# A two-layer decoder trunk in fp32: the split weights' rows and the low part of x at other offsets in memory

## Chip, cores and metric

One core of a Trainium2 chip (trn2) runs the whole program. The metric is the device time of one execution in microseconds (us), as a median of the runs shown. Engines: PE is TensorE (PEld its weight loads), DVE is VectorE, ACT is ScalarE, POOL is GpSimd, SP is the engine that issues most DMAs.

## What is computed

`x` is 512 tokens by 1024 features, fp32. Two layers, each: RMSNorm, one input projection, two mixers whose outputs are joined, an output projection, residual, RMSNorm, a squared-ReLU MLP of width 4096, residual. Layer 0 mixes with RWKV-7 and gated DeltaNet heads, layer 1 with top-k sparse and block-sparse attention.

```python
h = rms_norm(x, norm1_g[l])
x = x + mixer_l(h @ w_in) @ w_out          # w_in: 1024 x 3856 and 1024 x 2888; w_out: 1024 x 1024
h = rms_norm(x, norm2_g[l])
x = x + square(relu(h @ mlp_w1[l])) @ mlp_w2[l]   # 1024 x 4096, 4096 x 1024
```

## The kernel before

**A product in three passes.** A matmul in float32r keeps fewer bits than fp32, so both operands are split: `hi` is the value rounded to float32r, `lo` the rest. A weight tile times an activation is `w_hi*x_hi + w_lo*x_hi + w_hi*x_lo`. `products` (L535) issues it for the KT = 8 tiles of the contraction: first 8 pairs on the high activation (L542 with `w_hi`, L543 with `w_lo`), then 8 matmuls on the low activation (L547). The weight tile of 128 x 128 is the stationary operand, the 512 tokens are the moving one, and all 24 matmuls of such a group go to one PSUM bank.

**The input projection of layer 0** has weight tiles of 128 columns of its own (31 tiles, `tile` at L556, and `first_tiles` at L563 for two of them, with the same passes at L569, L570 and L574). Operands are `x_hi`, `x_lo`, `pw_hi`, `pw_lo`: PH, PL, PWH and PWL in the code. They are tensors laid over the arena by hand, at word offsets X_HI = 6696, PW_HI = 12968 and X_LO = 46704. An assert in the allocation ties these numbers to the carved regions.

**All later projections** take their weights in units of 256 columns (8 x 256 words in each of 128 partitions; there are 84). SP loads a unit into one of two raw slots (RAW), with rows of USLOT = 264 words. ACT rounds it into `w_hi` (`weight_hi`, L1163), POOL subtracts to get `w_lo` (`weight_lo`, L2313), each in two slots that take turns by `u % 2`, and PE runs one group of 24 matmuls for each half of 128 columns (`split_unit`, L895). ACT may fill a slot of `w_hi` when PE has finished the unit before last, and POOL follows ACT. 264 is there for one unit alone, `u_ikv`, which has 8 columns more. The activations are `a_hi`, `a_lo` (input of the MLP), `h_hi`, `h_lo` (input of the other projections and the hidden layer). In `token_major` (L991) of the value projections the sides are exchanged: the activation is stationary, and the weight rows of 256 or 136 columns move.

**Where the operands lie.** The slots and activations are allocated one behind the other:

```python
AH, AL, HL, HH = (parts(n_, 1, KT, W)[:, 0] for n_ in ("a_hi", "a_lo", "h_lo", "h_hi"))
WH, WL = parts("w_hi", 2, KT, USLOT), parts("w_lo", 2, KT, USLOT)
```

A word is 4 bytes, `lower` has 28224 words ahead of them, and W = 512. Counted from the start of `lower`, in bytes within 512:

| operand | start | step from one k to the next |
|---|---|---|
| a_hi, a_lo, h_lo, h_hi | 256 | 2048 (none within 512) |
| w_hi, w_lo, slot 0 | 256 | 1056 (32 within 512) |
| w_hi, w_lo, slot 1 | 0 | 1056 (32 within 512) |
| x_hi | 160 | 2048 (none) |
| pw_hi, pw_lo | 160 | 512 (none) |
| x_lo | 448 | 2048 (none) |

So the weight tile of step k stands 32*k bytes (plus 256 in slot 1) past the activation's place within 512 bytes, from 0 at k = 0 to 224 at k = 7. For layer 0's input projection that distance is 0 in the high passes, and 288 bytes in the low pass. The second half of a unit, 128 columns on, is 512 bytes further and so at the same place.

**Order of the work.** It is fixed by the program: each engine has its own list, and semaphores join them. PE waits for `lo_ready` before a unit and for `bank_read` before it writes a PSUM bank again; DVE empties the banks.

Of the kernel before, what the change touches and what calls it, by code (L numbers as in the profile page):

```python
# [25 lines left out]
ALU = mybir.AluOpType  # L26
# [71 lines left out]
def trunk_kernel(nc, a, out):  # L98
    ctx = ExitStack()
    with ctx:  # L100
# [1 line left out]
            return ctx.enter_context(nc.semaphore(name))  # L102

        ARENA, PARTS = 53000, 28224
        X_HI, PW_HI, X_LO = 6696, 12968, 46704
        with nc.sbuf_tensor("below_x_hi", [P, X_HI], F32), nc.sbuf_tensor("x_hi", [P, KT, W], F32R) as PH, \
                nc.sbuf_tensor("below_pw", [P, PW_HI - X_HI - KT * W], F32), \
                nc.sbuf_tensor("pw_hi", [P, 3, KT, P], F32R) as PWH, nc.sbuf_tensor("pw_lo", [P, 3, KT, P], F32R) as PWL:
# [9 lines left out]
        def parts(name, a_, n, w):  # L118
            return ctx.enter_context(nc.sbuf_tensor(name, [P, a_, n, w], F32R))

        AH, AL, HL, HH = (parts(n_, 1, KT, W)[:, 0] for n_ in ("a_hi", "a_lo", "h_lo", "h_hi"))
        WH, WL = parts("w_hi", 2, KT, USLOT), parts("w_lo", 2, KT, USLOT)
        ps = ctx.enter_context(nc.psum_tensor("ps", [P, 8, 512], F32))
        bank = [ps[:, i, :] for i in range(8)]

# [3 lines left out]
        def carve(n):  # L129
            off = top[0]  # L130
            top[0] += n
            assert top[0] <= ARENA, top[0]
            return off

        def flat(off, n):

            if off >= PARTS:
                return upper[:, off - PARTS:off - PARTS + n]
            assert off + n <= PARTS, (off, n)
            return lower[:, off:off + n]  # L140
# [66 lines left out]


        SQ_KKS = flat(carve(4 * PW), 4 * W)
        o_pl = carve(KT * W)  # L210
        PRAW = flat(o_ring, 2 * KT * P).rearrange("p (s k n) -> p s k n", s=2, k=KT)
        assert (X_HI, PW_HI, X_LO) == (o_ht, o_ring + 2 * KT * P, o_pl)
# [188 lines left out]
        def unit_cols(u):  # L401
            return USLOT if u == u_ikv else UW

        def as_f32(x):
            return x.bitcast(F32)

        x_rows = a["x"][0].rearrange("(t p) d -> p t d", p=P)

# [103 lines left out]
        def _(pe):  # L512
            def take(q, dyn=0):

                if q >= 8:
                    pe.wait_ge(bank_read, dyn + (q - 7))
                return bank[q % 8]
# [377 lines left out]
            def split_unit(u, q, xh, xl, dyn_u=0, dyn_q=0, waits=None, ks=tuple(range(KT))):  # L895

                pe.wait_ge(lo_ready, dyn_u + (u + 1))
                for b in range(2):
                    cols = slice(b * P, (b + 1) * P)
                    products(take(q + b, dyn_q)[:, :],  # L900
                             [(k, WH[:, u % 2, k, cols], WL[:, u % 2, k, cols], xh[:, k, :], xl[:, k, :])
                              for k in ks], waits if b == 0 else None).then_inc(bank_filled, 1)

            def normed_split(n):
# [17 lines left out]
            def mlp(l):  # L922
                def quarter(i, first):
                    for v in range(first, 4):
                        split_unit(u_mlp[l] + v, q_m1[l] + 2 * v, AH, AL, i * 8, i * 16)

                    hidden = (lambda k: pe.wait_ge(h1_hi, i * 8 + (32 * l + k + 1)),
                              lambda k: pe.wait_ge(h1_ready, i * 8 + (32 * l + 4 + k + 1)))
                    for v in range(4):
                        split_unit(u_mlp[l] + 4 + v, q_m2[l] + 2 * v, HH, HL, i * 8, i * 16,  # L930
                                   hidden if v == 0 else None)

                n, u = 2 * l + 1, u_mlp[l]
                pe.wait_ge(lo_ready, u + 1)
                sums, tile0, tile1 = take(q_norm[n]), take(q_m1[l]), take(q_m1[l] + 1)
                for k in range(KT):
                    pe.wait_ge(h_hi, KT * (n - 1) + k + 1)
                    for b, o in enumerate((tile0, tile1)):
                        cols = slice(b * P, (b + 1) * P)
                        pe.matmul(o[:, :], WH[:, u % 2, k, cols], AH[:, k, :], start=(k == 0), stop=False)  # L940
                        pe.matmul(o[:, :], WL[:, u % 2, k, cols], AH[:, k, :], start=False, stop=False)
                pe.wait_ge(sq_sum, sums_to(n + 1))
                pe.matmul(sums[:, :], ONES, SQ[n][:, 0, :], start=True, stop=True).then_inc(bank_filled, 1)
                for b, o in enumerate((tile0, tile1)):
                    cols = slice(b * P, (b + 1) * P)
                    for k in range(KT):
                        pe.wait_ge(h_lo, KT * (n - 1) + k + 1)
                        mm = pe.matmul(o[:, :], WH[:, u % 2, k, cols], AL[:, k, :], start=False,  # L948
                                       stop=(k == KT - 1))
                    mm.then_inc(bank_filled, 1)  # L950
                quarter(0, 1)
                if l == 0:
                    with pe.Fori(1, 4) as i:
                        quarter(i, 0)
                    return
                with pe.Fori(1, 3) as i:
                    quarter(i, 0)
                for v in range(4):
                    split_unit(u_mlp[l] + v, q_m1[l] + 2 * v, AH, AL, 24, 48)
                hidden = (lambda k: pe.wait_ge(h1_hi, 24 + (32 * l + k + 1)),  # L960
                          lambda k: pe.wait_ge(h1_ready, 24 + (32 * l + 4 + k + 1)))
                for v in range(3):
                    split_unit(u_mlp[l] + 4 + v, q_m2[l] + 2 * v, HH, HL, 24, 48, hidden if v == 0 else None)
                turned_tiles(0, range(4))
                u = u_mlp[l] + 7
                pe.wait_ge(lo_ready, 24 + (u + 1))
                for b in range(2):
                    cols = slice(b * P, (b + 1) * P)
                    products(take(q_m2[l] + 6 + b, 48)[:, :],
                             [(k, WH[:, u % 2, k, cols], WL[:, u % 2, k, cols], HH[:, k, :], HL[:, k, :])  # L970
                              for k in range(KT)]).then_inc(bank_filled, 1)
                    turned_tiles(1, range(2) if b == 0 else range(2, 4))

            def projected(l, xh, xl, waits, ks):
                for v in range(4):
# [9 lines left out]
            keep_busy(take(q_norm[2] + 1)[:, :], 5)  # L985
            u = u_ikv
            pe.wait_ge(lo_ready, u + 1)
            products(take(q_ik)[:, :], [(k, WH[:, u % 2, k, 0:P], WL[:, u % 2, k, 0:P], HH[:, k, :],
                                         HL[:, k, :]) for k in range(KT)], normed_split(2)).then_inc(bank_filled, 1)

            def token_major(o, i, wh, wl):  # L991

                rows = slice(i * P, (i + 1) * P)
                return products(o, [(k, HH[:, k, rows], HL[:, k, rows], wh[:, k, :], wl[:, k, :])
                                    for k in range(KT)])

            for v in range(2):
                o = take(q_v + v)
                for i in range(2):
                    mm = token_major(o[:, i * VIW:(i + 1) * VIW], 2 * v + i, WH[:, u % 2, :, P:USLOT],  # L1000
                                     WL[:, u % 2, :, P:USLOT])
                mm.then_inc(bank_filled, 1)

            def unit_tile(u, b, q):
                cols = slice(b * P, (b + 1) * P)
                pe.wait_ge(lo_ready, u + 1)
                products(take(q)[:, :], [(k, WH[:, u % 2, k, cols], WL[:, u % 2, k, cols], HH[:, k, :], HL[:, k, :])
                                         for k in range(KT)]).then_inc(bank_filled, 1)

            def mv(v):  # L1010
                u = u_mv[v]
                pe.wait_ge(lo_ready, u + 1)
                for i in range(TT):
                    token_major(take(q_mv[v * TT + i])[:, 0:UW], i, WH[:, u % 2, :, 0:UW],
                                WL[:, u % 2, :, 0:UW])\
                        .then_inc(bank_filled, 1)

            def index_products(i):
# [107 lines left out]
        def _(act):  # L1126
# [29 lines left out]
            def weight_hi(u, dyn=0, q_done=None, dyn_q=0):  # L1156


                act.wait_ge(raw_full[u % 2], dyn + raw_count(u))
                if q_done is not None:  # L1160
                    filled(q_done, dyn_q)
                w = unit_cols(u)
                act.activation(WH[:, u % 2, :, 0:w], RAW[:, u % 2, :, 0:w], ACT.Copy).then_inc(hi_ready, 1)  # L1163

            def h_split(n):
                for k in range(KT):
# [1035 lines left out]
        def _(pool):  # L2202
# [106 lines left out]
            def weight_lo(u, dyn=0):  # L2309

                pool.wait_ge(hi_ready, dyn + (u + 1))
                w = unit_cols(u)
                pool.tensor_tensor(WL[:, u % 2, :, 0:w], RAW[:, u % 2, :, 0:w],  # L2313
                                   as_f32(WH[:, u % 2, :, 0:w]), ALU.subtract)\
                    .then_inc(lo_ready, 1)

            def weights(first, last):
# [70 lines left out]
```

## Time and profile before

| | |
|---|---|
| median of 3 runs | 1460.98 us (1460.77 to 1461.29) |
| span of the profiled execution | 1458.6 us |
| what lies around the span, median less span | 2.4 us |
| PE busy | 1426.5 us, 98% of the span |
| PEld busy | 1140.5 us, 78% |
| DVE, ACT, POOL busy | 657.9, 595.2, 524.1 us |
| DMA | 110.06 MB, mean 75 GB/s |

The profile gives no time of its own for the profiled execution beside its span. A row of the page's list of groups names line, engine, operation, output and inputs, shape and count, then busy time, mean ns of one, and idle time before it with what ended it. Matmuls overlap: one is listed with some 390 ns from its start to its modelled end, while the next starts after some 230 ns. What a matmul costs in a full stream is therefore the spacing of the starts, to be read from the timeline, or from the chain of waits, where each matmul stands with the time until the next one took over.

### The profile page before, as it was taken

Reading aid. Unit: us, or ns where it says so; the run is one execution under the profiler, and the core shown is the slowest. Engines: PE = TensorE matmul, PEld = TensorE weight load, DVE = VectorE, ACT = ScalarE, POOL = GpSimd, SP = SyncE. Lnnn points to the kernel's source line nnn. Section 1 sums busy time; section 2 is a strip of 40 time slices with the busy share of each in tenths; the row PEclk is TensorE's granted clock in tenths of the full one; section 3 lists DMA queues with packets and bytes.
Section 4 is the critical chain, followed back from the end, with each engine's and each line's share of the span. In section 5 each row is a group of like instructions: output and inputs, shape, how many; then the busy total and the mean of one; then the engine's idle time right before and its main releaser. Section 6 shows DMA issues by size and latency. Waiting matters only on the chain.

```text
span 1458.6 us, 24642 instructions
## 1 busy us (share of the span) xinstructions
PE 1426.5 (98%) x10331; PEld 1140.5 (78%) x10331; DVE 657.9 (45%) x1090; ACT 595.2 (41%) x849; POOL 524.1 (36%) x239
## 2 busy tenths in 40 slices
PE   7999999999999999999999999999999999999998
PEld 5787778889787888888887767775687888888886
DVE  4665767788743214132133258836443223131231
ACT  5524663444634223133233465568635223131331
POOL 3543322011144334434444224332333533443341
PEclk9999999999999999999999999999999999999999
DMA  5333200000222322233223222210032223223221
GB/s 148 87 101 84 75 15 4 4 4 3 89 87 87 113 90 87 93 97 99 86 87 99 70 63 87 87 58 2 9 106 89 87 87 114 88 86 112 90 87 58
DMA packets 128972, 110.06 MB, mean 75 GB/s; under 512 B 10742, under 2 KB 126576, under 8 KB 128880
## 3 DMA queue, kind: packets, MB, share of 16 engines
q1 hardware_dynamic: 128000, 107.12, 23.7%
q8 instruction: 73, 1.20, 0.4%
q10 hardware_dynamic: 880, 1.59, 0.3%
q14 instruction: 19, 0.16, 0.0%
HBM read 106.60 MB, written 2.10 MB: 75 GB/s over the span
## 4 chain that ended last, share of the span: by engine, by line
PE 91%; DVE 4%; ACT 2%; POOL 1%; issue 1%; DMA 1%; SPq 0%; ACTq 0%; DVEq 0%; POOLq 0%
PE ps L547 24%; PE ps L542 24%; PE ps L543 24%; PE ps L679 5%; PE ps L1070 2%; PE ps L1080 1%; PE ps L1091 1%; PE ps L687 1%; PE ps L579 1%; PE ps L1045 1%; POOL pw_lo L2226 1%; PE ps L694 1%; PE ps L1021 1%; PE ps L656 1%; PE ps L948 1%
## 5 line engine op out<-in xcount | busy, mean ns | idle before, releaser
L2313 POOL TENSOR_TENSOR w_lo<-lower,w_hi 128x2048 fp32r<-128x2048 f32 (+1 forms) x84 | 388.8, 4629 | 551.0 <-ACT w_hi L1163 534.4
L542 PE MATMUL ps<-h_hi,w_hi 128*128 128x512 f32 x792 | 315.2, 398 | 0.9 <-ACT h_hi L1446 0.8
L543 PE MATMUL ps<-h_hi,w_lo 128*128 128x512 f32 x792 | 312.0, 394 | 0.0
L1163 ACT ACTIVATE w_hi<-lower 128x2048 fp32r<-128x2048 f32 (+1 forms) x84 | 160.2, 1907 | 242.8 <-PE ps L547 242.8
L547 PE MATMUL ps<-h_lo,w_hi 128*128 128x512 f32 x792 | 202.2, 396 | 0.5
L542 PE MATMUL ps<-a_hi,w_hi 128*128 128x512 f32 x480 | 189.1, 394 | 0.0
L543 PE MATMUL ps<-a_hi,w_lo 128*128 128x512 f32 x480 | 189.1, 394 | 0.0
L542 PEld LDWEIGHTS ps<-h_hi,w_hi 128*128 128x128 f32 x792 | 148.6, 188 | 41.7 <-issue 5.4
L547 PEld LDWEIGHTS ps<-h_lo,w_hi 128*128 128x128 f32 x792 | 148.7, 188 | 38.0 <-DVE h_lo L1770 2.5
L543 PEld LDWEIGHTS ps<-h_hi,w_lo 128*128 128x128 f32 x792 | 148.7, 188 | 35.6 <-issue 1.2
L2054 DVE TENSOR_TENSOR lower<-lower,ps 128x512 f32<-128x512 f32 x64 | 44.0, 687 | 275.4 <-PE ps L547 275.4
L2038 DVE SCALAR_TENSOR_TENSOR lower<-ps,lower 128x512 f32<-128x512 f32 x64 | 44.3, 692 | 226.0 <-PE ps L547 209.9
L1433 ACT ACTIVATE lower<-lower 128x512 f32<-128x512 f32 x64 | 40.5, 633 | 215.9 <-DVE lower L2038 215.9
L547 PE MATMUL ps<-a_lo,w_hi 128*128 128x512 f32 x480 | 121.5, 395 | 0.0
L2226 POOL TENSOR_TENSOR pw_lo<-lower,pw_hi 128x1024 fp32r<-128x1024 f32 (+1 forms) x31 | 73.6, 2376 | 111.2 <-ACT pw_hi L1175 111.0
L547 PEld LDWEIGHTS ps<-a_lo,w_hi 128*128 128x128 f32 x480 | 90.2, 188 | 21.7
L543 PEld LDWEIGHTS ps<-a_hi,w_lo 128*128 128x128 f32 x480 | 90.1, 188 | 21.4
L542 PEld LDWEIGHTS ps<-a_hi,w_hi 128*128 128x128 f32 x480 | 90.0, 188 | 21.1
L2043 DVE TENSOR_TENSOR h_lo<-lower,h_hi 128x512 fp32r<-128x512 f32 x64 | 97.4, 1521 | 6.9 <-ACT h_hi L1435 6.9
L542 PE MATMUL ps<-x_hi,pw_hi 128*128 128x512 f32 (+1 forms) x232 | 93.1, 401 | 0.4 <-POOL pw_lo L2226 0.4
L543 PE MATMUL ps<-x_hi,pw_lo 128*128 128x512 f32 (+1 forms) x232 | 90.7, 391 | 0.0
L679 PE MATMUL ps<-lower 64*64 64x64 f32 x2080 | 68.1, 220 | 3.6 <-DVE lower L1847 2.1
(386 smaller groups left out, 1889.1 us busy)
## 6 DMA issues: line engine op xcount, KB each, us to landing
lower<-in_mlp_w_dram SPq DMA_DIRECT2D x64, 1024.0 KB, 5.3
lower<-in_ev_w_in_dram SPq DMA_DIRECT2D x30, 512.0 KB, 3.8
lower<-in_od_w_in_dram SPq DMA_DIRECT2D x10, 1024.0 KB, 5.1
lower<-in_ev_w_out_dram SPq DMA_DIRECT2D x4, 1024.0 KB, 5.4
lower<-in_od_w_out_dram SPq DMA_DIRECT2D x4, 1024.0 KB, 4.9
lower<-in_od_w_in_dram SPq DMA_DIRECT2D x6, 256.0 KB, 3.8
out_dram<-lower SPq DMA_DIRECT2D x6, 256.0 KB, 2.6
upper<-in_x_dram SPq DMA_DIRECT2D x1, 1024.0 KB, 7.1
```

The costliest lines, as they stand in the source:

```text
L542: pe.matmul(o, wh, xh, start=(i_ == 0), stop=False)
L543: pe.matmul(o, wl, xh, start=False, stop=False)
L547: mm = pe.matmul(o, wh, xl, start=False, stop=(i_ == n_ - 1))
L679: mm = pe.matmul(ps[part, b, h_ * HD:(h_ + 1) * HD], mats[part, j, q, :], vals[part, j, q, :], start=(start and h_ == 0), stop=True, skip_ ...
L1070: pe.matmul(bank[n % 2 * 2 + p][:, 0:wdt], L1[part, b, rows], L1[part, 8 + b, 0:wdt], start=True, stop=True).then_inc(at_qk, 1)
L1163: act.activation(WH[:, u % 2, :, 0:w], RAW[:, u % 2, :, 0:w], ACT.Copy).then_inc(hi_ready, 1)
L1433: act.activation(sq, sq, ACT.Square).then_inc(h1_sq, 1)
L2038: dve.scalar_tensor_tensor(out=SQT[:, b % 4, :], in0=src(q)[:, :], scalar=0.0, in1=RS[2 * l + 1], op0=ALU.max, op1=mul).then_inc(bank_read, 1)
L2043: dve.tensor_tensor(HL[:, b, :], SQT[:, b % 4, :], as_f32(HH[:, b, :]), sub).then_inc(h1_ready, 1)
L2054: dve.tensor_tensor(XT[:, k, :], XT[:, k, :], src(q_m2[l] + k)[:, :], add)\
L2226: pool.tensor_tensor(PWL[:, u % 3, :, 0:w], PRAW[:, u % 2, :, 0:w], as_f32(PWH[:, u % 3, :, 0:w]), ALU.subtract).then_inc(pw_lo, 1)
L2313: pool.tensor_tensor(WL[:, u % 2, :, 0:w], RAW[:, u % 2, :, 0:w], as_f32(WH[:, u % 2, :, 0:w]), ALU.subtract)\
```

## The change

The tensors `w_hi` and `w_lo` keep their starts and sizes (2 slots of 8 * 264 words), but have no fixed row any more. `packed` takes the first 8 * w words of a slot as 8 rows of w columns, with w the unit's own number of columns: 256, and 264 for `u_ikv`. All that read or write the slots (PE, ACT, POOL) go by `w_high(u)` and `w_low(u)`. The raw slots keep rows of 264.

Then 56 words are carved ahead of the low part of x, so that `x_lo` starts at word 46760, with the four regions carved behind it (G2, WA, GD and the first RS) 56 words later too.

```diff
-        X_HI, PW_HI, X_LO = 6696, 12968, 46704
+        X_HI, PW_HI, X_LO = 6696, 12968, 46760
...
-        WH, WL = parts("w_hi", 2, KT, USLOT), parts("w_lo", 2, KT, USLOT)
+        WHB, WLB = (ctx.enter_context(nc.sbuf_tensor(n_, [P, 2, KT * USLOT], F32R)) for n_ in ("w_hi", "w_lo"))
...
         SQ_KKS = flat(carve(4 * PW), 4 * W)
+        carve(56)
         o_pl = carve(KT * W)
...
+        def packed(slots, u):
+
+            w = unit_cols(u)
+            return slots[:, u % 2, 0:KT * w].rearrange("p (k n) -> p k n", k=KT)
+
+        def w_high(u):
+            return packed(WHB, u)
+
+        def w_low(u):
+            return packed(WLB, u)
...
                 products(take(q + b, dyn_q)[:, :],
-                             [(k, WH[:, u % 2, k, cols], WL[:, u % 2, k, cols], xh[:, k, :], xl[:, k, :])
+                             [(k, w_high(u)[:, k, cols], w_low(u)[:, k, cols], xh[:, k, :], xl[:, k, :])
                               for k in ks], waits if b == 0 else None).then_inc(bank_filled, 1)
...
-                    mm = token_major(o[:, i * VIW:(i + 1) * VIW], 2 * v + i, WH[:, u % 2, :, P:USLOT],
-                                     WL[:, u % 2, :, P:USLOT])
+                    mm = token_major(o[:, i * VIW:(i + 1) * VIW], 2 * v + i, w_high(u)[:, :, P:USLOT],
+                                     w_low(u)[:, :, P:USLOT])
...
-                act.activation(WH[:, u % 2, :, 0:w], RAW[:, u % 2, :, 0:w], ACT.Copy).then_inc(hi_ready, 1)
+                act.activation(w_high(u)[:, :, 0:w], RAW[:, u % 2, :, 0:w], ACT.Copy).then_inc(hi_ready, 1)
...
-                pool.tensor_tensor(WL[:, u % 2, :, 0:w], RAW[:, u % 2, :, 0:w],
-                                   as_f32(WH[:, u % 2, :, 0:w]), ALU.subtract)\
+                pool.tensor_tensor(w_low(u)[:, :, 0:w], RAW[:, u % 2, :, 0:w],
+                                   as_f32(w_high(u)[:, :, 0:w]), ALU.subtract)\
```

In bytes within 512, the same table after the change:

| operand | start | step from one k to the next |
|---|---|---|
| w_hi, w_lo, slot 0 | 256 | 1024 (none within 512) |
| w_hi, w_lo, slot 1 | 0 | 1024 (none) |
| x_lo | 160 | 2048 (none) |

The slots begin where they did. For `u_ikv` nothing differs. No instruction is added, taken out or moved on any engine; the output of ACT's and of POOL's instruction for a unit is written as one run of 2048 words, where it was 8 rows of 256.

## Rows read from the trace of the kernel before

**Rows 1.** The page's first part: busy us, share of the span, instructions
```profile
PE 1426.5 (98%) x10331; PEld 1140.5 (78%) x10331; DVE 657.9 (45%) x1090; ACT 595.2 (41%) x849; POOL 524.1 (36%) x239
```

**Rows 2.** Two stretches (us from the start): busy us and (instructions) of each engine
```profile
core 0: us, PE busy (x) PEld busy (x) DVE busy (x) ACT busy (x) POOL busy (x), PEclk, DMA share, GB/s
500.00:700.00 200.00, 200.00 (x863) 161.62 (x862) 47.38 (x52) 53.37 (x50) 83.03 (x18) 1.00 0.30 97
1200.00:1400.00 200.00, 200.00 (x863) 161.66 (x862) 54.16 (x56) 58.47 (x58) 82.52 (x19) 1.00 0.30 95
```

**Rows 3.** Groups of 512-column matmuls in the projections (two parts of one list)
```profile
L542 PE MATMUL ps<-h_hi,w_hi 128*128 128x512 f32 x792 | 315.2, 398 | 0.9 <-ACT h_hi L1446 0.8
L542 PE MATMUL ps<-a_hi,w_hi 128*128 128x512 f32 x480 | 189.1, 394 | 0.0
L542 PE MATMUL ps<-x_hi,pw_hi 128*128 128x512 f32 x224 | 90.0, 402 | 0.4 <-POOL pw_lo L2226 0.4
...
L948 PE MATMUL ps<-a_lo,w_hi 128*128 128x512 f32 x32 | 8.6, 420 | 0.0
L569 PE MATMUL ps<-x_hi,pw_hi 128*128 128x512 f32 x16 | 6.3, 396 | 0.0
```

**Rows 4.** Timeline of PE in the first tiles: start us, us, instruction
```profile
14.24 0.40 PE L570 MATMUL ps<-x_hi,pw_lo 128*128 128x512 f32 x1
...
16.33 0.39 PE L569 MATMUL ps<-x_hi,pw_hi 128*128 128x512 f32 x1
...
21.09 0.39 PE L570 MATMUL ps<-x_hi,pw_lo 128*128 128x512 f32 x1
```

**Rows 5.** Chain of waits, input projection: start us, us, what
```profile
21.48 3.73 PE ps L574 x16
...
66.80 1.87 PE ps L547 x8
...
94.46 1.87 PE ps L547 x8
```

**Rows 6.** Chain of waits, MLP of layer 0
```profile
503.21 1.86 PE ps L547 x8
508.78 1.86 PE ps L547 x8
514.35 1.86 PE ps L547 x8
...
553.37 1.86 PE ps L547 x8
```

**Rows 7.** Timeline in one group of that MLP
```profile
501.89 0.39 PE L543 MATMUL ps<-h_hi,w_lo 128*128 128x512 f32 x1
502.12 0.39 PE L542 MATMUL ps<-h_hi,w_hi 128*128 128x512 f32 x1
502.34 0.40 PE L543 MATMUL ps<-h_hi,w_lo 128*128 128x512 f32 x1
502.58 0.40 PE L542 MATMUL ps<-h_hi,w_hi 128*128 128x512 f32 x1
```

**Rows 8.** Chain of waits, value projection with the weights moving
```profile
949.60 0.95 PE ps L547 x8
```

**Rows 9.** Timeline of ACT and POOL on one weight unit
```profile
499.53 1.92 ACT L1163 ACTIVATE w_hi<-lower 128x2048 fp32r<-128x2048 f32 x1 [7.23 <-PE ps L547]
...
501.52 4.60 POOL L2313 TENSOR_TENSOR w_lo<-lower,w_hi 128x2048 fp32r<-128x2048 f32 x1 [4.53 <-ACT w_hi L1163]
```

**Rows 10.** Chain of waits in the first 51 us: POOL and a DMA on it
```profile
35.08 2.41 POOL pw_lo L2226
...
50.98 5.25 DMA lower<-in_ev_w_in_dram
```

**Rows 11.** Waits of PE: us in total, times, longest
```profile
PE ps L583 <- DMA upper<-in_norm_g_dram: 5.8, 1, 5.8
...
PE ps L589 <- DMA upper<-in_x_dram: 2.4, 1, 2.4
...
PE ps L542 <- ACT h_hi L1446: 0.8, 1, 0.8
```

More of the change, by code:

```diff
@@ L939, in mlp @@
                         cols = slice(b * P, (b + 1) * P)
-                        pe.matmul(o[:, :], WH[:, u % 2, k, cols], AH[:, k, :], start=(k == 0), stop=False)
-                        pe.matmul(o[:, :], WL[:, u % 2, k, cols], AH[:, k, :], start=False, stop=False)
+                        pe.matmul(o[:, :], w_high(u)[:, k, cols], AH[:, k, :], start=(k == 0), stop=False)
+                        pe.matmul(o[:, :], w_low(u)[:, k, cols], AH[:, k, :], start=False, stop=False)
                 pe.wait_ge(sq_sum, sums_to(n + 1))
@@ L947, in mlp @@
                         pe.wait_ge(h_lo, KT * (n - 1) + k + 1)
-                        mm = pe.matmul(o[:, :], WH[:, u % 2, k, cols], AL[:, k, :], start=False,
+                        mm = pe.matmul(o[:, :], w_high(u)[:, k, cols], AL[:, k, :], start=False,
                                        stop=(k == KT - 1))
@@ L969, in mlp @@
                     products(take(q_m2[l] + 6 + b, 48)[:, :],
-                             [(k, WH[:, u % 2, k, cols], WL[:, u % 2, k, cols], HH[:, k, :], HL[:, k, :])
+                             [(k, w_high(u)[:, k, cols], w_low(u)[:, k, cols], HH[:, k, :], HL[:, k, :])
                               for k in range(KT)]).then_inc(bank_filled, 1)
@@ L987, in _ @@
             pe.wait_ge(lo_ready, u + 1)
-            products(take(q_ik)[:, :], [(k, WH[:, u % 2, k, 0:P], WL[:, u % 2, k, 0:P], HH[:, k, :],
+            products(take(q_ik)[:, :], [(k, w_high(u)[:, k, 0:P], w_low(u)[:, k, 0:P], HH[:, k, :],
                                          HL[:, k, :]) for k in range(KT)], normed_split(2)).then_inc(bank_filled, 1)
@@ L1006, in unit_tile @@
                 pe.wait_ge(lo_ready, u + 1)
-                products(take(q)[:, :], [(k, WH[:, u % 2, k, cols], WL[:, u % 2, k, cols], HH[:, k, :], HL[:, k, :])
+                products(take(q)[:, :], [(k, w_high(u)[:, k, cols], w_low(u)[:, k, cols], HH[:, k, :], HL[:, k, :])
                                          for k in range(KT)]).then_inc(bank_filled, 1)
@@ L1013, in mv @@
                 for i in range(TT):
-                    token_major(take(q_mv[v * TT + i])[:, 0:UW], i, WH[:, u % 2, :, 0:UW],
-                                WL[:, u % 2, :, 0:UW])\
+                    token_major(take(q_mv[v * TT + i])[:, 0:UW], i, w_high(u)[:, :, 0:UW],
+                                w_low(u)[:, :, 0:UW])\
                         .then_inc(bank_filled, 1)
```

## Prediction

> **What bounds the kernel now.** I read the page's first part, then PE's busy time by stretches, then the spacing of its matmuls. PE is busy for 98% of the span [rows 1]. That alone is weak evidence, because matmuls overlap in the listing. So I count starts: in 200 us of the MLPs PE runs 863 matmuls without a gap, in both layers, at a granted clock of 1.00, which is the 2.4 GHz level [rows 2]. That is 200 / 863 = 0.232 us each. Streaming 512 columns at 2.4 GHz takes 0.213 us, so about 19 ns of each matmul are something else. PE waits for nothing there; the longest wait of the whole kernel is 5.8 us for a load at the start, and the longest in these groups 0.8 us [rows 11]. The end is set by the spacing of these matmuls.
>
> **What that spacing follows.** The same form of matmul comes at three spacings.
>
> - First tiles, high pass, weights and activation at the same place within 512 bytes: 21 intervals from 16.33 to 21.09 us, 4.76 / 21 = 226.7 ns, and even [rows 4].
> - Low pass of the same tiles, distance 288 bytes: 3.73 / 16 = 233.1 ns; later tiles 1.87 / 8 = 233.8 ns, in every one [rows 5].
> - MLP, distance 32 bytes times k: groups of 24 follow each other by (553.37 - 503.21) / 9 = 5.573 us, that is 232.2 ns each; the low pass has 1.86 / 8 = 232.5 ns [rows 6]. Within a group the spacing is uneven in a way that repeats: 0.22 us after one matmul and 0.24 after the next [rows 7]. The groups of rows 6 take turns in slot 0 and slot 1, and in first and second half, and all have the same length, so 256 or 512 bytes more make no difference. 32 bytes times k does.
>
> The clock is the same in the three, and so are columns, rows and type. What differs is where the weight load reads while the matmul streams. I take 226.7 ns as the spacing that a stream keeps when both stand at the same place within 256 bytes, and the rest as the cost of being out of step. This is inferred from three places and the two differ in pass as well as in address, which the chances must carry.
>
> **Part 1, rows of 256 columns.** Each k now starts 1024 bytes on, so in slot 0 the weights stand where the activation stands, and in slot 1 256 bytes away, which the trace says is as good. The matmuls touched are 3 x (792 + 480) in the groups on h and a, and 3 x 32 in the opening of the MLPs, 3912 in all [rows 3]. Each goes from 232.2 to 226.7 ns: 3912 x 5.5 ns = 21.5 us. Two deductions. The 24 matmuls of the unit with 264 columns stay as they are: 0.1 us. After a stall the stream needs some matmuls to fall into step: in the first tiles the 9 intervals from 14.24 to 16.33 us took 2.09 us where 9 x 226.7 ns are 2.04 [rows 4], so 0.05 us a time. The timeline has about 18 stalls between these groups: 0.9 us. That leaves 20.5 us, all on the path, since PE is what everything else waits for.
>
> In the value projections the weight rows move, 256 columns in 0.95 / 8 = 119 ns [rows 8]. There are 192 of these. No row shows them in step. Bounds: nothing, or the 12 ns by which 119 exceeds 107 ns of streaming, 192 x 12 = 2.3 us. I take the share that the full ones gain (5.5 of 232, some 2.8 ns): 0.5 us. The 96 with 136 columns keep their layout.
>
> **Part 2, x_lo.** The low passes of 31 tiles: 15 x 16 = 240 matmuls of full width from 233.8 to 226.7 ns, 1.7 us. A high pass behind a low one now needs seven matmuls to fall into step: tiles follow each other by (94.46 - 66.80) / 5 = 5.532 us, less 1.87 for the low pass leaves 3.662 / 16 = 228.9 ns. If nothing falls out of step any more, 16 x 2.2 ns = 35 ns in each of 26 tiles, 0.9 us. Until 51 us POOL and a DMA are on the chain [rows 10], so what PE gains in the first four tiles is lost to waiting: 0.3 us off. Part 2 gives 2.3 us. The regions moved by 56 words feed 24 short-lived matmuls (L614, L618) and some ACT and DVE work at their own pace; I cost that at nothing, between 0.2 us won and 0.2 lost.
>
> **What hides the rest.** ACT's 1.92 us and POOL's 4.60 us for a unit have the same number of words as before, now written in one run. Should they slow down, the cover is this: ACT starts at 499.53 just after PE has left the slot's last user, POOL ends at 506.12 [rows 9], and PE wants the unit at 510.5, two groups of 5.57 us after 499.33. So 4.4 us are spare, 4.1 after the change, when a unit lasts 10.88 instead of 11.15 us. POOL would have to take nearly twice its time. The load of a raw slot is 5.3 us of a cycle of two units. Nothing else comes due earlier by more than 0.3 us a unit. No wait is added.
>
> **Sum.** 20.5 + 0.5 + 2.3 = 23.3 us. Against the profiled execution: 1458.6 - 23.3 = 1435.3 us of span; with the 2.4 us around it, 1437.7 us. The median shown is that span plus 2.4, so it stands in for the profiled execution's own time.
>
> **Rivals.**
>
> *Only half of it falls into step.* The matmuls at 226.7 ns are all of a high pass, in which an activation tile serves two weights. In a low pass every matmul has a new activation tile, and no low pass in the trace runs at 226.7. If the pass and not the address makes the 233.8 ns, each group keeps 8 x 233.8 and seven matmuls at 232.2 to fall into step, and only nine run at 226.7: 1.870 + 1.625 + 2.040 = 5.535 us instead of 5.573. Over 163 groups that is 6.2 us, part 2 gives nothing, and the time is 1454.8 us. Against it: the low pass of the first tiles repeats its uneven spacing for all 16 without settling, as if something constant held it out of step.
>
> *Addresses do nothing.* The 226.7 ns could come from the input projection's own surroundings, and the change would only rename rows: 1461 us. What speaks against it is that the spacing changes from 226.7 to 233 ns from one matmul to the next at 21.3 us, with the same weights. For this rival there is a rule. The Trainium skill, TensorE: Matmul & The Clock Gate, Step-by-step: what each phase is for, says that TensorE has two independent read ports into SBUF and that loading the next weights takes no read bandwidth from the running matmul. By that rule a relative offset could not matter and the sum would be 1461.0 instead of 1437.7; by the rows, the same weights at 226.7 and then 233 ns, something does collide. The same page, Back-to-back issue gap, gives an isolated matmul of 512 columns 512/2.4 + 2.5, about 216 ns; no stream of this kind here comes down to that.
>
> *A fixed offset locks the stream at the wrong value, and it is slower.* A constant distance of 288 bytes gave a constant 233.8 ns, worse than the 232.2 of the wandering one. If a stream at 256 bytes within 512, as h and a are, or at 256 bytes away, as slot 1 is, has such a state, then 3912 matmuls cost 1.6 ns more, 6.3 us, and with part 2's gain of at most 2.3 the time is 1465. It decides if the even state needs x's own place (160) and not just equality; slower than before begins where the h and a groups exceed 232.8 ns. Against it: slots 0 and 1 have equal groups now.
>
> *More than that.* If the moving rows could stream with nothing in between, the floor would be 213 ns, some 75 us less. No row of a full 128 x 128 weight load comes below 226.7, so this gets next to nothing.
>
> **How the numbers follow.** A measurement of this kernel can tell about 0.2%, 2.9 us, from no change. Full step 0.73; its own range is 1434 to 1443, where the lower end has the full 2.3 us of the value projections and no time lost after stalls, and the upper has one matmul in four still out of step. Half of it 0.13 (1454.8, faster too). No effect 0.07. Slower 0.05. More than forecast 0.02. The predicted time is that of the likeliest, 1437.7. The range goes from 1434 to 1456 and so takes in the second case. Faster 0.88, same 0.07, slower 0.05.
>
> **What would show it.** In the MLPs: 200 us hold 882 matmuls instead of 863; groups on L547 stand 5.44 us apart, the low pass of 8 takes 1.81 us, and the starts within a group are even. In the first tiles, L574 x16 takes 3.63 instead of 3.73 us, and the tiles behind are 5.44 us apart. The RWKV stretch from 220 to 398 us keeps its length. If the low passes stay at 1.86 or 1.87 us while the later part of the high pass is at 0.227, the second case holds. If slot 0 and slot 1 have groups of different length, equality within 256 bytes was the wrong rule. If POOL or ACT for a unit takes longer than 4.7 or 2.0 us, the way they are written matters. The forecast is wrong if the groups on h and a stay above 229 ns a matmul, or if PE, sped up, waits for `lo_ready`.

## The result and the profile after

The changed kernel takes 1436.26 us in the median of 4 runs, the kernel before 1460.88 us; the ratio is 0.9831, with a 95% interval of 0.9818 to 0.9845. (One of the four, at 6760 us with a granted clock of 0.20, was a disturbed one; the other three are between 1436.04 and 1436.35.) The prediction was 1437.7 us. In this section lines L5xx of before are 12 higher: L542, L543, L547 and L574 are now L554, L555, L559 and L586.

The page's first part answers to [rows 1]:

```profile
span 1434.3 us, 24642 instructions
PE 1401.7 (98%) x10331; PEld 1139.0 (79%) x10331; DVE 661.1 (46%) x1090; ACT 595.9 (42%) x849; POOL 526.0 (37%) x239
```

PE is 98% busy, as before, with the same number of instructions, and 24.8 us less of it. The share of busy time says nothing of the change; the number of matmuls in a stretch does. The stretches answer to [rows 2]:

```profile
core 0: us, PE busy (x) PEld busy (x) DVE busy (x) ACT busy (x) POOL busy (x), PEclk, DMA share, GB/s
500.00:700.00 200.00, 200.00 (x884) 165.67 (x883) 48.69 (x52) 53.97 (x50) 83.57 (x19) 1.00 0.31 99
1200.00:1400.00 200.00, 200.00 (x884) 165.58 (x884) 53.65 (x56) 57.17 (x55) 87.97 (x19) 1.00 0.29 95
```

884 matmuls in 200 us, where there were 863 at the same granted clock: one every 226.7 ns by the starts (the counts include those that reach over an edge of the stretch, so 200 / 884 comes out a little short). The chain of waits, input projection first and then the MLP of layer 0, answers to [rows 5, 6]:

```profile
20.95 3.63 PE ps L586 x16
65.69 1.81 PE ps L559 x8
71.13 1.81 PE ps L559 x8
...
502.65 1.81 PE ps L559 x8
508.09 1.81 PE ps L559 x8
513.53 1.81 PE ps L559 x8
```

3.63 us for 16 and 1.81 for 8 are 226.9 and 226.3 ns, in the low passes too, and groups stand 5.44 us apart in both places. The timeline inside a group answers to [rows 7]:

```profile
501.13 0.39 PE L554 MATMUL ps<-h_hi,w_hi 128*128 128x512 f32 x1
501.36 0.39 PE L555 MATMUL ps<-h_hi,w_lo 128*128 128x512 f32 x1
501.58 0.39 PE L554 MATMUL ps<-h_hi,w_hi 128*128 128x512 f32 x1
501.81 0.39 PE L555 MATMUL ps<-h_hi,w_lo 128*128 128x512 f32 x1
502.04 0.39 PE L554 MATMUL ps<-h_hi,w_hi 128*128 128x512 f32 x1
502.26 0.39 PE L555 MATMUL ps<-h_hi,w_lo 128*128 128x512 f32 x1
```

The uneven steps of 0.22 and 0.24 us are gone; these five are 0.226 us each. One place got worse, the value projection with the weights moving [rows 8]:

```profile
934.41 0.96 PE ps L559 x8
```

It had 0.95 us. From the starts of the 192 such matmuls the mean spacing went from 118.6 to 119.9 ns. ACT and POOL kept their times for a unit: the means of the 84 are 1911 and 4645 ns, against 1907 and 4629.

**Where the 24.3 us of span came from.** The matmuls come in the same order in both kernels, so their starts can be set side by side. First and last rows of the stretches, before:

```profile
13.93 0.48 PE L569 MATMUL ps<-x_hi,pw_hi 128*128 128x512 f32 x1
...
210.40 0.59 PE L705 MATMUL ps<-upper,lower 128*128 128x512 f32 x1
...
398.06 0.47 PE L542 MATMUL ps<-h_hi,w_hi 128*128 128x512 f32 x1 [0.79 <-ACT h_hi L1446]
...
1453.10 0.65 PE L917 MATMUL ps<-lower 128*128 128x128 f32 x4 [0.34 <-DVE lower L2054]
```

and after:

```profile
13.43 0.48 PE L581 MATMUL ps<-x_hi,pw_hi 128*128 128x512 f32 x1
...
207.29 0.59 PE L717 MATMUL ps<-upper,lower 128*128 128x512 f32 x1
...
394.47 0.47 PE L554 MATMUL ps<-h_hi,w_hi 128*128 128x512 f32 x1 [0.79 <-ACT h_hi L1458]
...
1428.76 0.66 PE L929 MATMUL ps<-lower 128*128 128x128 f32 x4 [0.34 <-DVE lower L2066]
```

Until the input projection ends, 210.40 - 207.29 = 3.1 us are won, of which 0.5 were there at the first projection matmul already (13.93 against 13.43 us, loads that landed sooner in this execution). Then 0.5 in the RWKV and DeltaNet stretch, where 187.66 became 187.18 us, and from there to the last transposes (1453.10 - 398.06) - (1428.76 - 394.47) = 20.75 us.

### The profile page after: what moved, and what is told of

Same layout as the page of the kernel before. It is cut to its first block, busy times and chain, and to the rows that moved or that the text cites. A ratio compares the mean times of both kernels' runs of the same rounds, so it can differ in the third digit from the quotient of the medians.

```text
span 1434.3 us, 24642 instructions
## 1 busy us (share of the span) xinstructions
PE 1401.7 (98%) x10331; PEld 1139.0 (79%) x10331; DVE 661.1 (46%) x1090; ACT 595.9 (42%) x849; POOL 526.0 (37%) x239
## 4 chain that ended last, share of the span: by engine, by line
PE 90%; DVE 4%; ACT 2%; POOL 1%; issue 1%; DMA 1%; SPq 0%; ACTq 0%; DVEq 0%; POOLq 0%
PE ps L554 24%; PE ps L559 24%; PE ps L555 24%; PE ps L691 5%; PE ps L1082 2%; PE ps L1092 1%; PE ps L1103 1%; PE ps L699 1%; PE ps L591 1%; PE ps L1057 1%; POOL pw_lo L2238 1%; PE ps L706 1%; PE ps L1033 1%; PE ps L668 1%; PE ps L960 1%
## 5 line engine op out<-in xcount | busy, mean ns | idle before, releaser
L2325 POOL TENSOR_TENSOR w_lo<-lower,w_hi 128x2048 fp32r<-128x2048 f32 (+1 forms) x84 | 390.2, 4645 | 529.4 <-ACT w_hi L1175 513.4
L554 PE MATMUL ps<-h_hi,w_hi 128*128 128x512 f32 x792 | 311.8, 394 | 0.9 <-ACT h_hi L1458 0.8
L555 PE MATMUL ps<-h_hi,w_lo 128*128 128x512 f32 x792 | 308.4, 389 | 0.0
L1175 ACT ACTIVATE w_hi<-lower 128x2048 fp32r<-128x2048 f32 (+1 forms) x84 | 160.5, 1911 | 235.2 <-PE ps L559 235.1
L559 PE MATMUL ps<-h_lo,w_hi 128*128 128x512 f32 x792 | 197.2, 390 | 0.5
L554 PE MATMUL ps<-a_hi,w_hi 128*128 128x512 f32 x480 | 186.7, 389 | 0.0
L555 PE MATMUL ps<-a_hi,w_lo 128*128 128x512 f32 x480 | 186.7, 389 | 0.0
L554 PEld LDWEIGHTS ps<-h_hi,w_hi 128*128 128x128 f32 x792 | 148.7, 188 | 38.3 <-issue 5.4
L559 PEld LDWEIGHTS ps<-h_lo,w_hi 128*128 128x128 f32 x792 | 148.7, 188 | 33.1 <-DVE h_lo L1782 2.5
L555 PEld LDWEIGHTS ps<-h_hi,w_lo 128*128 128x128 f32 x792 | 148.7, 188 | 31.5 <-issue 1.2
L559 PE MATMUL ps<-a_lo,w_hi 128*128 128x512 f32 x480 | 118.5, 389 | 0.0
L554 PEld LDWEIGHTS ps<-a_hi,w_hi 128*128 128x128 f32 x480 | 90.1, 188 | 18.7
L559 PEld LDWEIGHTS ps<-a_lo,w_hi 128*128 128x128 f32 x480 | 90.1, 188 | 18.7
L555 PEld LDWEIGHTS ps<-a_hi,w_lo 128*128 128x128 f32 x480 | 90.1, 188 | 18.7
L2055 DVE TENSOR_TENSOR h_lo<-lower,h_hi 128x512 fp32r<-128x512 f32 x64 | 100.8, 1575 | 7.1 <-ACT h_hi L1447 7.1
L554 PE MATMUL ps<-x_hi,pw_hi 128*128 128x512 f32 (+1 forms) x232 | 92.7, 400 | 0.5 <-POOL pw_lo L2238 0.5
L555 PE MATMUL ps<-x_hi,pw_lo 128*128 128x512 f32 (+1 forms) x232 | 90.4, 390 | 0.0
```

The source lines that it names most:

```text
L554: pe.matmul(o, wh, xh, start=(i_ == 0), stop=False)
L555: pe.matmul(o, wl, xh, start=False, stop=False)
L559: mm = pe.matmul(o, wh, xl, start=False, stop=(i_ == n_ - 1))
L1175: act.activation(w_high(u)[:, :, 0:w], RAW[:, u % 2, :, 0:w], ACT.Copy).then_inc(hi_ready, 1)
L2055: dve.tensor_tensor(HL[:, b, :], SQT[:, b % 4, :], as_f32(HH[:, b, :]), sub).then_inc(h1_ready, 1)
L2325: pool.tensor_tensor(w_low(u)[:, :, 0:w], RAW[:, u % 2, :, 0:w], as_f32(w_high(u)[:, :, 0:w]), ALU.subtract)\
```

## Experiments

**The two parts apart.** `rows_only` is the changed kernel with the old place of x_lo:

```diff
-        X_HI, PW_HI, X_LO = 6696, 12968, 46760
+        X_HI, PW_HI, X_LO = 6696, 12968, 46704
...
-        carve(56)
```

> Part 1 alone: slots as rows of 256 columns, x_lo back at 448 within 512. Address theory: the groups on h and a keep 5.44 us, the low passes on x_lo are back at 233 to 234 ns a matmul and the high passes behind them need seven matmuls to fall into step; 1436.2 plus some 3 us, 1439.2 us. If x_lo's place did nothing (the gain in the input projection came from elsewhere), 1436.2 us.

`xlo_only` is the kernel before with these lines the other way round, so that x_lo moves and the rows of 264 stay.

> Part 2 alone: rows of 264 as before, x_lo at 160 within 512. Address theory: the input projection runs at 226.7 ns throughout, the groups on h and a stay at 5.57 us; 1460.9 less some 3 us, 1457.9 us. If the two parts need each other or x_lo's place did nothing: 1460.9 us.

`rows_only` took 1439.03 us against 1460.37 (ratio 0.9854, 0.9839 to 0.9869), `xlo_only` 1457.48 (0.9987, 0.9972 to 1.0002, an interval that touches no change). In stretches, first `rows_only` and then `xlo_only`:

```profile
51.00:220.00 169.00, 165.05 (x782) 126.07 (x782) 114.18 (x153) 84.09 (x118) 63.40 (x28) 1.00 0.25 69
500.00:700.00 200.00, 200.00 (x884) 165.58 (x884) 49.44 (x53) 53.89 (x50) 86.15 (x19) 1.00 0.29 95
```

```profile
51.00:220.00 169.00, 165.03 (x801) 127.90 (x801) 116.28 (x156) 84.48 (x120) 65.10 (x30) 1.00 0.25 72
500.00:700.00 200.00, 200.00 (x863) 161.68 (x862) 47.85 (x52) 53.42 (x50) 82.89 (x18) 1.00 0.30 95
```

Each part acts in its own stretch and leaves the other as it was: 884 against 863 in the MLP for the rows. (The counts of 51:220 also hold short matmuls of the next stretch, so they are not to be compared.) In the input projection the starts show the old pattern with `rows_only` (a mean of 233 to 234 ns in the low pass, seven uneven matmuls behind it, tiles of 5.533 us) and, behind a stall's first few matmuls, 226.7 ns with `xlo_only` (5.440 us), whose chain of waits has

```profile
67.12 1.81 PE ps L548 x8
72.56 1.81 PE ps L548 x8
```

21.3 and 2.9 us add up to 24.2, where both together won 24.6, so the parts are independent within what these times can tell. In `xlo_only` it is the activation that moved while the weights stayed.

**A constant distance that is not zero.** The change does two things at once: the distance from the activation's place becomes the same for every k, and it becomes 0 (or 256 bytes). To tell these apart, `dist32` puts the rows 8 words later in their slots, and `dist128` 32 words (`(32, 32)` in place of `(8, 8)`):

```diff
-        def packed(slots, u):
+        def packed(slots, u, shifts):
 
             w = unit_cols(u)
-            return slots[:, u % 2, 0:KT * w].rearrange("p (k n) -> p k n", k=KT)
+            s = shifts[u % 2] if w == UW else 0
+            return slots[:, u % 2, s:s + KT * w].rearrange("p (k n) -> p k n", k=KT)
...
-            return packed(WHB, u)
+            return packed(WHB, u, (8, 8))
...
-            return packed(WLB, u)
+            return packed(WLB, u, (8, 8))
```

> As the change, but every unit of 256 columns stands 8 words later in its slot, so the weights are always 32 bytes past the activation's place (plus 256 in slot 1), the same for every k. Theory A (equal place within 256 bytes is what counts): a constant distance of 32 bytes costs what 288 bytes cost x_lo before, 233 to 234 ns a matmul; 3912 matmuls times 6.8 ns on top of 1436.2 is 1463 us, slower than the kernel before. Theory B (only constancy from k to k counts, and any constant distance falls into step): 226.7 ns, 1436 us.

> As dist32 with 32 words, a constant distance of 128 bytes, as far from 0 and 256 as it can be. Theory A in its plain form: out of step as well, between 229 and 236 ns a matmul, 1445 to 1473 us. If what counts is a period of 128 bytes and not of 256: 226.7 ns and 1436 us. Theory B: 1436 us.

`dist32` took 1461.75 us against 1460.37 (ratio 1.0010, 1.0001 to 1.0019), `dist128` 1458.21 (0.9996, 0.9977 to 1.0016). The chain of waits of `dist32`:

```profile
500.86 1.87 PE ps L560 x8
506.45 1.87 PE ps L560 x8
512.05 1.87 PE ps L560 x8
517.65 1.87 PE ps L560 x8
```

Groups of 5.60 us, 233.3 ns a matmul, with the low pass at 1.87 us as x_lo had it at its 288 bytes before. Constancy from k to k is worth nothing by itself: theory B falls. `dist128` has groups of 5.577 us in the mean, no better than the wandering distance. 32 bytes, and nothing else, turn a gain of 24 us into a small loss. `dist32` also answers a rival that the prediction did not name: ACT and POOL write each unit as one run here too, so the way it is written is not what gained. Nor is it a collision with these writes: ACT's 1.9 us fall into the first group of a unit alone, and both groups of a unit have the same 5.600 us.

**Other distances, and one weight out of step.** The next three carry two distances each, one for each slot, so that one run gives two readings (`(16, 48)`, `(4, 24)` and `(60, 2)` words in place of `(8, 8)`). `lo32` moves w_lo alone, with `(0, 0)` for w_hi and `(8, 8)` for w_lo.

> Constant distances, one for each slot: 16 words in slot 0 (64 bytes) and 48 words in slot 1 (192, with the slot's own 256 it is 448 bytes). Read from each slot's own groups. Theory A (only 0 within 256 bytes is in step): both slots between 232 and 233.5 ns a matmul, groups of 5.57 to 5.60 us, time near 1460 us. Rival (a shorter period or a smooth fall with distance): one of them at 5.44 us, or both clearly apart from each other, time between 1436 and 1450 us.

> Constant distances of 16 bytes in slot 0 and 96 bytes in slot 1. Theory A: slot 1 as the others, 5.57 to 5.60 us a group. Slot 0 tells how near to equal the places must be: if any difference breaks the step, 5.58 us; if 16 bytes are still the same place, 5.44 us. Time near 1460 us in the first case, near 1449 us in the second.

> Constant distances of 240 bytes in slot 0 (16 short of 256) and 8 bytes in slot 1. If the rule is nearness to a multiple of 256 in either direction, slot 0 behaves as 16 bytes does. If it is exact equality, both slots have groups of 5.57 to 5.60 us, 1460 us. If nearness within 16 bytes is enough, 1436 us.

> w_hi as in the change (in step), w_lo alone 32 bytes further. In the high pass every second weight load is at distance 0 and every second at 32; the low pass uses w_hi alone. Theory A with a cost that each load has by itself: high pass 16 times 230 ns, low pass seven matmuls to fall into step and then 226.7, groups of 5.53 us, 1452 us. Rival (one load out of step throws the stream out for all of the high pass): 16 times 232 to 233 ns, groups of 5.57 us, 1459 us.

They took 1456.23, 1462.92, 1444.39 and 1458.79 us in a single execution each, the kernel before 1460.77. For `dist16_96` theory A holds: both slots are out of step (5.60 and 5.62 us). `dist64_192` fits neither expectation. Its slot 0, at 64 bytes, has 5.60 us throughout, but in slot 1, at 192 bytes, every second unit is faster than the next. Of its chain of waits, the two groups of one such unit and the two of the next:

```profile
500.03 1.83 PE ps L560 x8
505.52 1.83 PE ps L560 x8
...
522.29 1.87 PE ps L560 x8
527.89 1.87 PE ps L560 x8
```

5.49 us and 5.60 us apart, with the same offsets in both. This goes on through both MLPs, so a distance alone does not fix the spacing; what else does was not tried. `dist240_8` was the surprise. Its chain of waits, with slots that take turns every two rows:

```profile
504.40 1.85 PE ps L560 x8
509.88 1.81 PE ps L560 x8
515.32 1.82 PE ps L560 x8
520.83 1.84 PE ps L560 x8
526.36 1.85 PE ps L560 x8
```

5.48, 5.44, 5.51 and 5.53 us apart: groups in slot 0, at 240 bytes, run in step, though only 16 bytes at the other side (16 bytes, in slot 0 of `dist16_96`) are fully out of step. In `lo32` the high pass is uneven and slow although every second weight load is at distance 0 (columns as before, from the timeline):

```profile
502.02 0.40 PE L555 MATMUL ps<-h_hi,w_hi 128*128 128x512 f32 x1
...
505.30 2.00 PE L560 MATMUL ps<-h_lo,w_hi 128*128 128x512 f32 x8
507.14 0.40 PE L555 MATMUL ps<-h_hi,w_hi 128*128 128x512 f32 x1
```

In the rows of `lo32`, 14 matmuls in 3.28 us are 234 ns each; the low pass, with w_hi alone, takes 1.84 us for 8, 230 ns, and comes back to 227 only at its last two. So the cost does not belong to single loads: the stream as a whole is in step or not, and takes six or seven matmuls to get there. The rival of that run holds.

**How far the place in step reaches.** Two more runs, with `(56, 1)` and `(62, 52)` words, were to find the edges of a window around 240:

> Constant distances of 224 bytes in slot 0 and 4 bytes in slot 1. 240 bytes were in step and 16 were not, so the window of places in step lies at and below a multiple of 256. If it reaches 32 bytes down, slot 0 has groups of 5.44 us; if it ends at 16, 5.50 us or more. 8 bytes above cost 230.7 ns a matmul, so 4 should cost between 227 and 230.7: groups of 5.44 to 5.54 us in slot 1.

> Constant distances of 248 bytes in slot 0 and 208 bytes in slot 1. Between 240 and 256 all should be in step: slot 0 at 5.44 us. 192 had 231.3 ns and 240 had 226.7, so 208 should lie between, groups of 5.46 to 5.55 us in slot 1. If it is a step and not a slope, 208 behaves as 192, 5.55 us.

They took 1459.98 and 1461.24 us in a single execution each. There is no window: 224 and 248 bytes are at 5.60 us, and 4 bytes, at 5.58, are slower than the 5.44 to 5.54 expected. Only 208 bytes came out as one branch of its expectation had it. All distances together, from the starts of 32 groups from some 482 us on (the length of a group, and a 24th of it; distances in slot 1 have the slot's own 256 bytes on top):

| distance, bytes | slot | group, us | ns a matmul |
|---|---|---|---|
| 0 (the change) | both | 5.440 | 226.7 |
| 4 | 1 | 5.58 | 232.4 |
| 8 | 1 | 5.54 | 230.8 |
| 16 | 0 | 5.60 | 233.4 |
| 32 | both | 5.60 | 233.3 |
| 64 | 0 | 5.60 | 233.2 |
| 96 | 1 | 5.62 | 234.3 |
| 128 | both | 5.577 | 232.4 |
| 192 | 1 | 5.50 and 5.60, unit by unit in turn | 229.2 and 233.4 |
| 208 | 1 | 5.56 | 231.8 |
| 224 | 0 | 5.60 | 233.2 |
| 240 | 0 | 5.442 | 226.8 |
| 240 (`dist240`, below) | both | 5.440 | 226.7 |
| 248 | 0 | 5.60 | 233.3 |
| 32 * k (before) | both | 5.573 | 232.2 |

Of twelve constant distances other than 0 ten lie between 230.8 and 234.3 ns, 192 has two values, 229.2 and 233.4, and one, 240, is as good as 0 in these groups. Most of them were tried in one slot and one execution only. `dist240` asked whether it is a place of its own, with 60 words in both slots:

> A constant distance of 240 bytes in both slots. In the run that mixed it with 8 bytes it kept 226.7 ns, while 224 and 248 were out of step at 233.3. If 240 is a place in step like 0, all groups take 5.44 us and the time is that of the change, 1436.3 us within 1 us. If it only held because of the slot it took turns with, groups are at 5.5 us or more and the time is 1450 us or more.

The groups came out by the first half of the expectation, the time by neither. It took 1443.79 us in the median (1437.38 to 1450.75, 4 executions; before 1460.46, ratio 0.9878, 0.9835 to 0.9922). In the profiled execution, 1445.9 us of span, nearly all groups are 5.44 us, but seven in the first stretch on h (from 400 to 433 us, granted clock 1.00) keep 5.48 to 5.50, until a stall ends them; so at this one distance a stream can stay at 228.3 ns as well as at 226.7. The change has 5.44 there. And some 10 us went elsewhere, in the stretch of the second norm:

```profile
800.00:850.00 50.00, 49.06 (x204) 41.16 (x202) 5.76 (x9) 13.90 (x19) 13.77 (x3) 0.76 0.24 63
850.00:880.00 30.00, 29.57 (x139) 21.54 (x140) 22.61 (x36) 16.82 (x31) 10.24 (x5) 1.00 0.12 36
```

The granted clock is 0.76 in the mean of these 50 us, and the 136-column matmuls start every 0.21 us instead of 0.11: the 1.2 GHz level instead of 2.4. Ahead of it PE had waited for the normed tiles. The kernel before passes the same wait at 1.00. Two of the four executions, this one and the one of 1450.75 us, have a granted clock of 0.99 in the mean; the other two, at 0.998, took 1437.38 and 1439.98 us, against 1436.04 to 1436.35 for the change. Other distances have such an execution too: `xlo_only` one of 11 (1468.72 us, 0.99) and `dist128` one of 10 (1472.41 us, 0.99), 11 and 14 us above their medians. Whether 240 bytes make it more frequent was not tried.

**A version that should beat both.** In the value projection the sides are exchanged, and `dist64_192` had shown 113.5 ns a matmul for its slot 1 where the change has 119.9. `mv192` shifts those two units alone, and POOL's loop is unrolled for them:

```diff
-            return slots[:, u % 2, 0:KT * w].rearrange("p (k n) -> p k n", k=KT)
+            s = 48 if u in u_mv else 0
+            return slots[:, u % 2, s:s + KT * w].rearrange("p (k n) -> p k n", k=KT)
...
-            weights(u_mq, u_out[1])
+            weights(u_mq, u_mv[0])
+            for u in u_mv:
+                weight_lo(u)
```

> The change, with the two units of the MoBA values (weights moving, activation stationary) alone 48 words later in their slots; POOL's loop over three pairs of units is written as two pairs and two single units. Theory: there the weight load reads the activation and the stream reads w, and the distance that suits is another: the run with 192 bytes in slot 1 showed 113.5 ns a matmul, the change 119.9. With 192 bytes in both slots 192 matmuls save 6.4 ns each, 1.2 us: 1435.0 us. Rival (what helped was slot 1's own 256 bytes together with 192): half of it, 1435.6 us.

It took 1435.89 us against 1460.18, ratio 0.9835 (0.9821 to 0.9848); the change has 0.9831. The chain of waits at the same place:

```profile
934.54 0.94 PE ps L560 x8
937.37 0.94 PE ps L560 x8
```

117.8 ns in the mean of the 192, so 0.4 us won and not 1.2, which no measurement of the time here can tell. Slot 1 had the very distance of `dist64_192` and ran at 118 ns, not 113.5. So here too the spacing depends on more than the distance, as in the full groups at 192 bytes. It may be the state in which the stream arrives; that was not tried.

## Why the prediction was right

**Right.** The mechanism, its place and its size. The matmuls on h and a went from 232.2 to 226.7 ns, the floor that the first tiles had shown [rows 4]. Part 1 was put at 20.5 us for the full matmuls and 0.5 for the value projection; the stretch that holds both gave 20.75, which is 21.0 from the matmuls on h and a less 0.25 lost in the value projection. Part 2 was put at 2.3 us; from the first to the last projection matmul (3.1 less the 0.5 at the start) it gave 2.6. Stalls: the mean spacing of the 3874 matmuls on h and a that are followed within 300 ns is now 226.82 ns, so falling into step costs 0.6 us, where 0.9 was put. POOL and ACT had the same times as before, and the list of PE's waits has none for `w_lo` or `w_hi`. That the 256 bytes of slot 1 and the 512 of a second half make no difference, which was read from equal groups [rows 6], holds after the change in both slots.

**Off in size.** The value projection: 0.5 us of gain was taken by the share of the full matmuls, and it lost 0.25 (192 times 1.3 ns). The step at fault is "I take the share that the full ones gain": there the stationary side is the activation, and distance 0 is not its best place (119.9 ns, against 116.7 at 32 bytes). The RWKV stretch was said to keep its length and was 0.5 us shorter; the same 0.5 us came at the start without any cause in the change, so this is within what two executions differ by (the kernel before has 1459.14 to 1461.77 us over 27). The 1.0 us by which the span beat the sum is made of these two and of 0.5 more in the full matmuls and 0.3 more in part 2, less the 0.75 by which the value projection missed. The time agrees to 0.1% partly because these cancel. The lower end of the range, 1434, is 1 us below what its two terms give (1437.7 - 1.8 - 0.9 = 1435.0); nothing hangs on it.

**The rivals.** That only the high pass would fall into step is refuted by 1.81 us in every low pass, and by `xlo_only`. That addresses do nothing is refuted by `dist32`: same instructions, same clock, 32 bytes, 25.5 us more than the change. The prediction drew this rival from the Trainium skill, TensorE: Matmul & The Clock Gate, Step-by-step: what each phase is for, by which loading the next weights takes no read bandwidth from the running matmul. These runs do not agree with what was drawn from it: the place that the load reads changes the spacing of the matmuls from 226.7 to 233.3 ns. Whether read bandwidth is the reason, they do not show. The slower rival described something real, only not for this change: a constant distance can be worse than the wandering one. It needed a distance such as 32 bytes, and then 1461.75 us came of it, near the 1463 that the same 233 to 234 ns had given as an expectation. What it feared, that the even state needs x's own place and not just equality, did not occur: operands at 160 and operands at 256 both run at 226.7 ns.

**What stays open.** Why a stream out of step costs 4 to 8 ns more was not settled. The runs show that the distance between what the weight load reads and what the matmul streams changes it, whether the weights are moved (`dist32`) or the activation (`xlo_only`), and that the stream keeps a state over several matmuls. At distance 0 every group settled at 226.7 ns; 240 bytes did so too in nearly all of its groups, while 248 and 224 did not. The distance does not settle it alone: 192 bytes gave 229.2 and 233.4 ns in turn, and 240 bytes 226.7 and 228.3. That the two reads collide in memory is the simplest reading of it, and was argued, not shown.

## What to carry to other kernels

In a stream of full matmuls with a new weight tile each, try a row pitch of the weights that is a multiple of 256 bytes (here 512 and 1024 were run), and put weights and moving operand at the same place within 256 bytes. Here 8 columns of padding for the sake of one unit cost 1.5% of the kernel. Read the spacing of starts and not busy time, and look for a stretch where the same matmul runs faster; it shows the floor, and here the difference between the two stretches was an address. After such a fix keep to distance 0: another distance that is as good in most groups of one trace (240 bytes) held some groups at 5.48 us, and none of its four executions was as short as the change. And look at single groups before trusting a mean: the 5.55 us of 192 bytes is a group that never occurs.

## What the runs showed of the hardware that was not expected

- Constant distances other than 0 gave 230.8 to 234.3 ns a matmul, with two exceptions among twelve: 240 bytes at 226.8, and 192 bytes, where units at 229.2 and at 233.4 ns take turns. Closeness does not help: 4, 8 and 248 bytes are 4 to 7 ns worse than 0.
- One of two alternating weight tensors out of place (`lo32`) throws the whole high pass out of step, 234 ns, and the next six or seven matmuls too.
- With the activation stationary and 256 weight columns moving, the order is another: 119.9 ns at distance 0, 118.6 with the wandering distance, 116.7 at 32 bytes, and 113.5 or 118 at 192 bytes in the same slot in two kernels. `dist128` has 119.9 in one slot and 118.6 in the other at the same distance.
- With `dist240` the granted clock fell to the 1.2 GHz level behind the wait at the second norm and cost some 10 us. The other profiled executions did not lose it there, but one unprofiled execution each of `xlo_only` and `dist128` was as slow, with a granted clock of 0.99.
